# A hybrid attention / pooling / PEER step on one core: the second half of a tile's dense gates leaves one weight chunk later in the SyncE queue

## The reference, cut to what matters

```python
def peer(h, wq, keys, u, v):
    q = (x @ wq).reshape(t, PEER_HEADS, 2, PEER_HALF)
    sc = jnp.einsum('thpc,hpnc->thpn', q, keys).astype(jnp.float32)
    s_top, i_top = lax.top_k(sc, PEER_TOPK)
    cand = (s_top[:, :, 0, :, None] + s_top[:, :, 1, None, :]).reshape(t, PEER_HEADS, PEER_TOPK * PEER_TOPK)
    cs, ci = lax.top_k(cand, PEER_TOPK)
    ...
    idx = i1 * PEER_N_KEYS + i2
    g = jax.nn.softmax(cs, axis=-1).astype(h.dtype)
    ...
        a = jnp.einsum('thkd,td->thk', u[ii], xi)
        act = jax.nn.gelu(a, approximate=False) * gi
        return jnp.einsum('thk,thkd->td', act, v[ii])
```

## Time and profile before

| What | Value |
|---|---|
| Median of the three runs | 3332.68 us |
| The three runs | 3329.0, 3338.2, 3332.68 us |
| The profiled execution | span 3328.8 us; its own time is not listed apart from the three |
| PE busy | 3155.1 us (95%) |
| DVE busy | 2920.0 us (88%) |
| POOL busy | 1959.7 us (59%) |
| ACT busy | 1085.0 us (33%) |
| Moved by DMA | 1061.65 MB |

### The profile page before, as it was taken

One profiled execution on the slowest core, in us unless ns is written; L12 is line 12 of the kernel. 1 busy time (PEld: TensorE's weight loads), 2 busy tenths in 40 slices (PEclk: granted clock), 3 DMA queues, 4 the chain that ended last, 5 costly groups with the idle time before them and its releaser, 6 DMA issues.

```text
span 3328.8 us, 49532 instructions
## 1 busy us (share of the span) xinstructions
PE 3155.1 (95%) x15562; PEld 2568.4 (77%) x15562; DVE 2920.0 (88%) x5511; ACT 1085.0 (33%) x1661; POOL 1959.7 (59%) x1479
## 2 busy tenths in 40 slices
PE   7898998889999999999999799969999999999998
PEld 4455555558999999999998446649999999999997
DVE  2754298897999999999999699999999999999998
ACT  3122123333333333333333323333333333333333
POOL 0000045666777887777775037667777877777773
PEclk9999999989999999999999799979999999999998
DMA  5131265579999999999997264569999999999995
GB/s 210 51 127 54 93 261 233 237 297 393 407 403 410 401 408 385 408 409 409 392 402 307 101 253 202 202 249 396 408 410 400 404 401 388 402 395 409 410 408 222
DMA packets 249112, 1061.65 MB, mean 319 GB/s; under 512 B 23104, under 2 KB 73024, under 8 KB 205376
## 3 DMA queue, kind: packets, MB, share of 16 engines
q0 software_dynamic: 147456, 536.94, 40.8%
q1 hardware_dynamic: 101568, 523.63, 39.9%
HBM read 1007.26 MB, written 53.22 MB: 319 GB/s over the span
## 4 chain that ended last, share of the span: by engine, by line
PE 77%; DVE 12%; issue 5%; DMA 4%; ACT 1%; DVEq 0%; POOL 0%; SPq 0%; POOLq 0%; ACTq 0%
PE bankA L1338 10%; PE bankA L1340 10%; PE bankA L1339 10%; PE bankD L1351 6%; PE bankD L1352 6%; PE bankD L1350 6%; PE bankA L1292 4%; PE bankD L1260 3%; PE bankA L1352 3%; PE bankA L1351 3%; PE bankA L1350 3%; PE bankA L1433 3%; PE bankD L1479 2%; DMA wch<-in_wq 2%; DVE wch L1135 1%
## 5 line engine op out<-in xcount | busy, mean ns | idle before, releaser
L1338 PE MATMUL bankA<-hh,uh 128*128 128x384 f32 x2048 | 688.6, 336 | 29.0 <-DVE ul L1119 29.0
L1340 PE MATMUL bankA<-hh,ul 128*128 128x384 f32 x2048 | 688.8, 336 | 0.0
L1339 PE MATMUL bankA<-hl,uh 128*128 128x384 f32 x2048 | 687.4, 336 | 0.0
L573 POOL DMA_INDIRECT hT<-in_v,idxc x320 | 463.6, 1449 | 177.4 <-issue 68.9
L573 POOL DMA_INDIRECT hT<-in_u,idxc x320 | 461.6, 1443 | 166.6 <-issue 88.1
L699 ACT ACTIVATE wt<-bankA 128x384 f32<-128x384 f32 x256 | 126.0, 492 | 1046.9 <-PE bankA L1340 1046.8
L539 POOL TENSOR_TENSOR mask<-mask,topf 128x1024 f32<-128x1024 f32 x36 | 84.4, 2366 | 605.6 <-DVE mask L1045 605.6
L1338 PEld LDWEIGHTS bankA<-hh,uh 128*128 128x128 f32 x2048 | 385.9, 188 | 38.9 <-issue 29.1
L1135 DVE SCALAR_TENSOR_TENSOR wch<-hT,a,wch 128x1024 f32<-128x1024 f32 x320 | 399.8, 1281 | 11.4 <-DMA hT<-in_v,idxc 11.3
L1351 PE MATMUL bankD<-vl,wh 128*128 128x512 f32 x1024 | 399.8, 390 | 0.0
L1352 PE MATMUL bankD<-vh,wl 128*128 128x512 f32 x1024 | 399.3, 390 | 0.0
(11 more groups left out here) (202 smaller groups left out, 5621.9 us busy)
## 6 DMA issues: line engine op xcount, KB each, us to landing
uraw<-in_uT SPq DMA_DIRECT2D x128, 1024.0 KB, 11.7
vraw<-in_vP SPq DMA_DIRECT2D x128, 1024.0 KB, 7.9
wch<-in_wq SPq DMA_DIRECT2D x40, 2048.0 KB, 8.1
wch<-in_ada SPq DMA_DIRECT2D x24, 2048.0 KB, 8.1
gates_scratch<-gbuf SPq DMA_DIRECT2D x12, 4096.0 KB, 11.8
wch<-gates_scratch SPq DMA_DIRECT2D x64, 768.0 KB, 16.4
wch<-in_qkv SPq DMA_DIRECT2D x3, 2048.0 KB, 8.2
hT<-in_u,idxc POOLq DMA_INDIRECT x320, 10.3
```

Of the source, the lines that this page charges most:

```text
L573: pool.indirect_dma_start(out=row_buf[slot], out_offset=None, in_=table.rearrange("l e d -> (l e) d"), in_offset=bass.IndirectOffsetOnAxis ...
L1338: pe.matmul(abank[c], hi, hh[:, k, :], start=k == 0, stop=False)
L1339: pe.matmul(abank[c], hi, hl[:, k, :], start=False, stop=False)
L1340: last = pe.matmul(abank[c], lo, hh[:, k, :], start=False, stop=k == K - 1)
```

## The change

Each half of a tile's gates gets its own entry in `behind`. The first half stays where it was, behind the load of c1. The second half of tiles 0 and 1 (`unit[2] < DT - 1`) moves behind the load of c2, in both layers. For tile 2, the last with dense gates, both halves stay behind c1. `store_gates` stores one half per call, with the same wait and the same semaphore as before. Nothing else changes, on no other engine.

```diff
             elif unit[0] == "gates":
-                behind.append((len(chunks) + 1, unit[2]))
+                for half in range(2):
+                    behind.append((len(chunks) + 1 + (half if unit[2] < DT - 1 else 0), unit[2], half))
         LAST_LOAD[len(chunks) - 1] = L
-        for n, t in behind:
-            STORES.setdefault(min(n, len(chunks) - 1), []).append((L, t))
+        for n, t, half in behind:
+            STORES.setdefault(min(n, len(chunks) - 1), []).append((L, t, half))
...
-            def store_gates(L, t):
-
-                for half in range(2):
-                    n = (L * DT + t) * 2 + half
-                    sp.wait_ge(g_out, (n + 1) * (TB // HOT) + 2)
-                    sp.dma_start(gates_d[2 * t + half], gbuf[:, half, :, :]).then_inc(stored[half], 16)
+            def store_gates(L, t, half):
+
+                n = (L * DT + t) * 2 + half
+                sp.wait_ge(g_out, (n + 1) * (TB // HOT) + 2)
+                sp.dma_start(gates_d[2 * t + half], gbuf[:, half, :, :]).then_inc(stored[half], 16)
...
-                for L, t in STORES.get(n, []):
-                    store_gates(L, t)
+                for L, t, half in STORES.get(n, []):
+                    store_gates(L, t, half)
```

## The result

| | before | changed |
|---|---|---|
| Median | 3332.27 us (7 runs) | 3340.84 us (7 runs) |
| Range of the runs | 3329.0 to 3338.2 us | 3338.02 to 3343.99 us |
| Ratio, 95% interval | | 1.0026 (1.0016 to 1.0036) |
| Span of the profiled execution | 3328.8 us | 3336.2 us |
| Routing, layer 0: PE's gates of tile 0 / 1 / 2 start | 492.8 / 579.9 / 666.0 us | 493.0 / 579.2 / 664.7 us |

The change costs 8.6 us. It was forecast at -0.4 us. The time lies just inside the stated range (3326 to 3341 us), but the loss is clear of the measurement and wasn't foreseen. The starts of the gates, read from PE's timelines, place it: layer 0's routing comes out even at its end, all of the loss is in layer 1's.

The account below looks back on a forecast made before the run. PE, busy 95% of the span, was taken to wait in routing for loads behind the gates' store. Layer 0's -4.2 us plus layer 1's +2.1 and +1.7 gave -0.4, so 3332.3 us from a 3332.7 median; range 3326 to 3341 us.

Parts of the forecast that it names:

- What bounds the kernel: Routing stages: c2's load queued behind the gates' store makes PE wait, 8.95 us in layer 0, 3.17 and 4.25 in layer 1.
- the clock's price: PE's unit behind a wait runs at a lower granted clock: 10.4 us, against 8.1 us without a wait.
- Nothing else pays for the moved store: The store landing some 12 us later costs ACT nothing, and SP is not held up before c3's load.
- I take the same totals in the new order, as the bytes are the same: c2, store and c3 together take 22.8 us in layer 0, 22.3 and 23.4 in layer 1, from c2's issue.
- c2 lands after 8.1 us: Layer 0: c2's load, issued at 530.9, lands at 539.0, 0.2 us after PE has ended c1.
- All of it passes on: Layer 0: the 2.1 us gained per tile reaches the next gates in full, 4.2 us for tiles 0 and 1.
- nothing catches the gain: End of layer 0's routing, paced by PE and by loads, keeps the whole 4.2 us gain.
- Layer 1: mechanism: c3's later landing makes PE wait before c3's unit, losing 2.1 us at tile 0 and 1.7 us at tile 1.
- "Slower": Rival at c3's load, four times: the store holds c3 up 3.2 us more per tile, 12.8 us, 3345 us; chance 0.06.
- Overtaking: Rival: c3's load overtakes the store and follows c2 at once, some 24.6 us faster, 3308 us; chance 0.03.
- "The moved store does nothing": Rival: c2 lands as late as now, PE waits where it does now; 3332.7 us or up to 4 more; chance 0.06.
- The clock kept its price: Rival: PE keeps its clock through the new waits, four units 2.3 us shorter, -9.2 us, 3323 us; chance 0.09.

Follow-up runs that it names:

- the run that held the store back: Changed kernel, but SP holds the second half's store of tiles 0 and 1 until c2 has landed: ratio 1.0042, 3343.11 us.
- the early store: Kernel before, but for tiles 0 and 1 the second store resends the first half of `gbuf` as soon as that is done: 0.9949, 3314.68 us.

## Why the prediction was wrong, point by point

**What bounds the kernel: right.** A load behind the store ended PE's wait, and with the store out of the way layer 0 is 18 to 20 us shorter from tile 0's gates to tile 2's. So was the clock's price: 10.4 us forecast for a unit behind a wait, 10.1, 10.4 and 11.2 measured before c3. Not forecast was that c2's unit in layer 0 would be slow as well (10.1 us); it costs nothing, since c3's landing ends the next wait anyway.

**Nothing else pays for the moved store: right.** ACT's idle time before its copies into `gbuf` ended with PE's gates (105.5 us in all, 105.7 before) and not with a store, and SP issued c3 at 539.0, as PE ended c1.

**"I take the same totals in the new order, as the bytes are the same": the step that failed.** It was forecast as 22.8, 22.3 and 23.4 us from c2's issue to c3's landing; it was 24.2 in layer 0, and 24.5 and 24.1 in layer 1 (2039.0 to 2063.5, 2119.6 to 2143.7). The range I had kept for it, up to 26.0, held all of them; I took its lower end as the value. The runs show which part of the total it was. c3 lands 4.9 us behind the transfer in front of it in both orders, all four times. The pair in front is what grew: from the first issue to the second landing, store and then c2 took 17.9 us in layer 0, 17.4 and 18.5 in layer 1; c2 and then the store takes 19.4 and 19.5 in layer 0, 19.6 and 19.2 in layer 1. "Full queue, same bytes, same total" left out that a pair can take longer in one order than in the other. Why it does is open: in the old order the two issues also lay further apart (1.2 to 6.2 us, now 0.4), and no run separates the order from the distance. Worked through the forecast's own account, 1.4 us more per tile in layer 0 leaves 0.7 us of the 2.1 forecast; the gates of tiles 1 and 2 came 0.9 and 0.6 us closer to those before them.

**"c2 lands after 8.1 us": too low.** It took 9.5 to 9.9 us with the store right behind it, and the run that held the store back shows the store to be the cause (7.9 us). That cost PE some 1.5 us of waiting ahead of c2's unit, but these only shorten the wait before c3, which ends at the same landing.

**"All of it passes on", "nothing catches the gain": wrong.** The 1.2 us by which tile 2's gates were early in layer 0 were gone at the first matmul of experts; of 17.9 us with the early store 15.3 were left, of 18.5 us with the store behind c5 17.2. Layer 0's account was -4.2 us, measured about 0. The PE timelines have the ada units at the end at either clock, 1.92 or 3.64 us, according to how their waits fall; I hadn't looked at that stretch.

**Layer 1: mechanism right, size wrong.** Forecast +3.8 us (2.1 and 1.7), measured +8.3. From the end of tile 0's gates to the start of tile 1's, PE took 45.0 us instead of 40.3, 4.7 more (2.8 forecast); from tile 1's to tile 2's 45.5 instead of 42.1, 3.4 more (1.7 forecast). Of these 3.6 us over the forecast 2.9 are c3's later landings (2.2 and 0.7), the rest is the 11.2 us unit behind tile 1 (0.8). In that execution tile 0's gates also took 0.8 us longer; the kernel with layer 1 alone changed has 36.2 us for them, as before, and makes the same loss with 4.9 and 3.9 us between the gates.

**The sum.** Layer 0 was 4.2 us too good, layer 1 4.5 us: 8.7 of the 9.0 us between the forecast -0.4 and the measured +8.6. A sum of two terms of opposite sign that nearly cancel was only as good as their one common input, and that error had one sign in all four tiles: it took from the gain and added to the loss. That belonged in the chances. "Slower" had 0.06 from a rival that needed 2.6 us per tile to pass 10 us; c3 came 0.7 to 2.2 us later than forecast and the time came to 8.6.

**The rivals.** The slower one named the right place and sign, at too high a price. Overtaking fell: c3 landed 4.8 us behind the store. "The moved store does nothing" fell as well. The clock kept its price.

## What to carry to other kernels

A transfer that stands in front of loads that an engine waits for has to be moved past all of those that are needed before the next stretch without need of loads; moved by one, two or three places it only hands the wait on, here at -1.4, -0.6 and +5.2 us (the last two from one execution each), against -18.4 us at the fourth. Look for the place by listing, for each load behind the candidate place, when its consumer will want it. Where the engine has slack over a shorter wait (layer 1), leave it alone: the swap makes two waits out of one and takes a slow clock from one unit to the next.

## What the runs showed of the hardware that I had not expected

- On one queue, a 2 MB load with a 4 MB store issued 0.4 us behind it landed after 9.5 to 9.9 us instead of 7.9 to 8.2. The store behind it landed 19.0 us after its issue, 9.8 us after the load. The landings keep the order of issue, but what stands behind a load still slows it. The price isn't the same everywhere: behind tile 1 in layer 1 the load takes 8.7 to 8.9 us with nothing right behind it (in four of the experiments), and 9.5 with the store; what slows it there wasn't looked into.
- The Trainium skill, "DMA: Bandwidth & Descriptors", section "Queues, rings and completion order", says that on one ring a later descriptor may finish its write before an earlier one. The landings here are of whole transfers, and those kept the order of issue in every case read, store before load and load before store; no run shows the order of single descriptors.
- With a query unit behind it, a wait of 3.17 to 8.95 us costs some 2 to 3 us more on that unit: it takes 9.7 to 11.2 us in the two kernels, the longest behind 4.25 and 5.85 us, where one without a wait takes 8.1. Behind 1.98 us it was there in full (10.1 us at 0.83); behind the waits of 1.87 us it wasn't seen (a unit of 8.4 us at a clock of 1.00):

```profile
540.88:549.30 8.42, 8.42 (x28) 4.21 (x28) 8.15 (x26) 1.17 (x2) 4.02 (x2) 1.00 0.98 421
```
